# Identity products in TensorE's waits of a two-layer diffusion transformer with experts

## What is computed

```python
for l in range(2):                       # 256 latent tokens x, 256 context tokens xc, width 1024
    sh1, sc1, g1, sh2, sc2, g2 = modulation(c, w_ada[l], b_ada[l])      # silu(c) @ (1024 x 6144), also for c_ctx
    h_lat = rmsnorm(x, norm1_g[l]) * (1.0 + sc1) + sh1                  # the same for h_ctx
    o_lat, o_ctx = mixer(h_lat, h_ctx, ...)    # w_in; attention, 8 heads of 64; conv of 31 taps; w_out
    x = x + g1 * o_lat                   # xc likewise in layer 0 only
    h_lat = rmsnorm(x, norm2_g[l]) * (1.0 + sc2) + sh2
    f_lat = swiglu(h_lat, ...) if l == 0 else moe_swiglu(h_lat, ...)    # layer 1: top 2 of 8 experts
    x = x + g2 * f_lat
return rmsnorm(x, final_g)
```

## Time and profile before

| what | us |
|---|---|
| median of 3 runs | 1485.72 |
| lowest and highest | 1484.06 and 1485.72 |
| the profiled execution | 1484.85 |
| its span, first to last instruction | 1483.0 |
| TensorE busy in the span | 1384.1 |
| DMA rate over the span, GB/s | 266 |

### The profile page before, as it was taken

One profiled execution on the slowest core, in us unless ns is written; L12 is line 12 of the kernel. 1 busy time (PEld: TensorE's weight loads), 2 busy tenths in 40 slices (PEclk: granted clock), 3 DMA queues, 4 the chain that ended last, 5 costly groups with the idle time before them and its releaser, 6 DMA issues.

```text
span 1483.0 us, 25756 instructions
## 1 busy us (share of the span) xinstructions
PE 1384.1 (93%) x11327; PEld 821.8 (55%) x11327; DVE 525.7 (35%) x954; ACT 398.7 (27%) x701; POOL 4.1 (0%) x8
## 2 busy tenths in 40 slices
PE   6899889999999999989898999999999998889886
PEld 3688657888888888878675343333333332223221
DVE  2799884523232333469864112011100010001022
ACT  3522485422222322376482111010110010000001
POOL 0000000000000000000000000000000000000010
PEclk9999899999999999999999999999999999999898
DMA  9997903532331052411418999999999999999995
GB/s 353 385 343 274 352 2 114 171 114 68 103 114 57 29 187 97 143 57 58 171 41 341 399 371 409 406 409 406 409 407 408 408 406 410 405 410 406 408 410 221
DMA packets 147031, 395.92 MB, mean 267 GB/s; under 512 B 7488, under 2 KB 38752, under 8 KB 146912
## 3 DMA queue, kind: packets, MB, share of 16 engines
q1 hardware_dynamic: 144000, 388.86, 68.7%
q10 hardware_dynamic: 2336, 3.24, 0.6%
q0 software_dynamic: 576, 2.10, 0.4%
HBM read 390.76 MB, written 3.41 MB: 266 GB/s over the span
## 4 chain that ended last, share of the span: by engine, by line
PE 77%; DMA 12%; DVE 6%; SPq 2%; ACT 2%; issue 1%; DVEq 0%; ACTq 0%
PE bank L1196 22%; DMA weight_ring<-in_exp_w 9%; PE bank L1154 8%; PE bank L1013 5%; PE bank L1014 5%; PE bank L1012 5%; PE bank L735 4%; PE bank L736 4%; PE bank L737 4%; DMA weight_ring<-in_w_ada 3%; PE bank L1021 3%; PE bank L1022 3%; PE bank L1023 3%; PE bank L1162 2%; PE bank L681 2%; DVE weight_ring L1865 2%
## 5 line engine op out<-in xcount | busy, mean ns | idle before, releaser
L1196 PE MATMUL bank<-weight_ring,gathered 128*32 128x512 f32 (+1 forms) x3840 | 402.2, 569 | 32.9 <-DMA weight_ring<-in_exp_w 27.1
L1196 PEld LDWEIGHTS bank<-weight_ring,gathered 128*32 128x32 f32 x3840 | 127.0, 112 | 283.0 <-issue 282.3
L2259 DVE TENSOR_TENSOR scratch<-scratch,bank 64x512 f32<-64x512 f32 (+1 forms) x60 | 38.4, 640 | 357.2 <-ACT scratch L1672 354.9
L1154 PE MATMUL bank<-weight_ring,scratch 128*32 128x512 f32 x1344 | 157.8, 593 | 2.2 <-DMA weight_ring<-in_exp_w 2.2
L1014 PE MATMUL bank<-slot_halves,slot_halves 128*128 128x512 f32 x336 | 130.9, 390 | 0.0
L1013 PE MATMUL bank<-hT_halves,slot_halves 128*128 128x512 f32 x336 | 130.9, 390 | 0.0
L1012 PE MATMUL bank<-slot_halves 128*128 128x512 f32 x320 | 124.8, 390 | 0.0
L1865 DVE SCALAR_TENSOR_TENSOR weight_ring<-scratch,conv_weights,weight_ring 128x512 f32<-128x512 f32 (+1 forms) x207 | 121.3, 637 | 2.6 <-ACT weight_ring L1453 0.7
L736 PE MATMUL bank<-hT_halves,slot_halves 128*128 128x512 f32 (+1 forms) x352 | 122.0, 347 | 0.0
L735 PE MATMUL bank<-slot_halves,slot_halves 128*128 128x512 f32 (+1 forms) x284 | 105.6, 372 | 8.1 <-DVE slot_halves L1772 5.2
L1154 PEld LDWEIGHTS bank<-weight_ring,scratch 128*32 128x32 f32 x1344 | 43.8, 110 | 100.3 <-issue 91.0
(11 more groups left out here) (303 smaller groups left out, 1576.1 us busy)
## 6 DMA issues: line engine op xcount, KB each, us to landing
weight_ring<-in_exp_w SPq DMA_DIRECT2D x216, 1024.0 KB, 18.5
weight_ring<-in_w_ada SPq DMA_DIRECT2D x24, 2048.0 KB, 13.5
weight_ring<-in_exp_w SPq DMA_DIRECT2D x64, 768.0 KB, 15.0
weight_ring<-in_ffn_w SPq DMA_DIRECT2D x33, 1024.0 KB, 5.4
weight_ring<-in_w_in SPq DMA_DIRECT2D x8, 1024.0 KB, 11.6
weight_ring<-in_w_out SPq DMA_DIRECT2D x4, 2048.0 KB, 11.2
weight_ring<-in_w_in SPq DMA_DIRECT2D x2, 3072.0 KB, 15.2
expert_rows<-scratch ACTq DMA_DIRECT2D x14, 128.0 KB, 6.0
```

Of the source, the lines that this page charges most:

```text
L1154: i = mm(bank[6][quarter, :], at01[:, c0:c0 + BLOCK], w2[:, i_, half * 512:(half + 1) * 512], start=(first and i_ == 0), stop=(last and i_ ...
L1196: i = mm(ps[BLOCK * job:BLOCK * (job + 1), 0:cw], gathered_block(e, k, b), w[:, kk, a * cw:(a + 1) * cw], start=(k == 0), stop=(k == KT - 1))
```

## The change

A new function multiplies the 128 x 128 identity by itself into a PSUM bank that nobody reads; 105 such products stand at twelve places of TensorE's queue. Nothing waits for them and they wait for nothing, except that in the attention of both layers a wait on `roped` (third query or key tile rotated) stands ahead of them, since their bank held that tile's result. The other engines' queues are unchanged.

```diff
+            def keep_clock(n, ps):
+                for _ in range(n):
+                    mm(ps[:, 0:P], ident, ident, start=True, stop=True)
...
                     turn_first(1)
+                    keep_clock(9, bank[2])
                     first_modulation(3)
                     turn_first(2)
                     turn_first(3)
+                    keep_clock(18, bank[2])
                 else:
+                    keep_clock(6, bank[7])
                     norm_broadcast(4, TT)
+                    keep_clock(11, bank[7])
...
                 score(0)
                 for st in range(len(U) + 2):
+                    if st == 1:
+                        keep_clock(8, bank[4])
                     if st + 1 < len(U):
                         score(st + 1)
                     if st == 0:
+                        pe.wait_ge(m["roped"], 3)
+                        keep_clock(10 if l else 5, bank[4])
...
                         nk = 4 - U[p][2]
+                        if p == 0 and l == 0:
+                            keep_clock(7, bank[4])
...
+                if l:
+                    keep_clock(6, bank[7])
                 norm_broadcast(3 * l + 3, TQ)
+                if l:
+                    keep_clock(5, bank[7])
...
                 for u in range(ROW_UNITS[CH - 1]):
+                    keep_clock(3, bank[2])
                     second_unit(r, NG - 1, u)
```

## The result

The changed kernel takes 1486.8 us (median of 22 runs, 1483.6 to 1490.3); the kernel before, on the same chip, 1484.4 us (22 runs, 1482.8 to 1486.7). The ratio is 1.0016, 95% interval 1.0009 to 1.0022: it is **slower by 2.4 us**, where 1481.6 us were forecast and 1485.6 us was the upper end of the range. The profiled execution of after took 1485.67 us, its span is 1483.9 us.

What follows compares the result with a forecast made beforehand. It took DMA to bound the start and the experts' stream, with half-clock TensorE stretches costing time elsewhere; +1.4 + 0 - 1.25 - 1.8 - 0.7 - 0.9 = -3.25 us on 1484.85 gave 1481.6 us, range 1478.2 to 1485.6.

Steps and rivals of the forecast that it cites:

- The price of a product: All places: 0.225 us for each further product, up to 0.29 us each with the start, 0.45 us at half clock.
- rival C: All places: products don't hold the clock and are in the way at half clock; sum +5.2, 1490.0 us; chance 0.10.
- Start, +1.4 us: 9 and 18 products fit, but their lead ends at the w_ada transfer; half clock follows the new wait: +1.4 us.
- Rival A: Start: the clock holds behind the new wait at 71.45 us, start worth -0.3 us, total 1479.9 us; chance 0.17.
- rival B: Start: the early gain passes because the transfer lands sooner, -3.0 instead of +1.4, total 1477.2 us; chance 0.08.
- Attention of layer 0, 0 us: 5, 8, 7 products: gain at most 1.2 us, cost 0.6 us on VectorE's chain; taken as 0, bounds -0.6 and +0.8.
- rule against the forecast: Transposes don't engage the full clock; if identity products were treated alike, all gains would be nought.
- Entry to layer 1, -1.25 us: 6 and 11 products hidden in waits; the projection's first products reach ScalarE sooner: -1.25 us, bounds -1.4 and 0.
- Attention of layer 1, -1.8 us: 10 and 8 products hidden in waits; full clock brings the convolution's mean sooner: -1.8 us, bounds -2.4 and -0.6.
- Entry to the experts, -0.7 us: 6 and 5 products hidden in waits; the router's 32 records end sooner: -0.7 us, bounds -0.9 and 0.
- Tail, -0.9 us: 3 products ahead of each of the last four units remove half clock: -0.9 us, bounds -1.5 and +0.5.
- Rival D: Late places: products help, but dips move to other waits; half the late gains, 2.3, total 1483.9 us; chance 0.23.

Runs made afterwards that it cites:

- e2: The kernel before with only the 9 and 18 products of the start: 1487.6 us against 1484.2 us, ratio 1.0025.
- e9: The kernel before with 216 satisfied waits (108 instructions) in TensorE's idle places at the start, no products: 1487.1 us against 1484.6 us, ratio 1.0016.
- e3: The kernel before with only layer 0's 5, 8 and 7 attention products and their wait: 1487.2 us, ratio 1.0021.
- e7: e1 with 13 more products in layer 1's waits near 688 and 759 us: 1481.5 us against 1484.4 us, ratio 0.9981.
- e6: The kernel before with 108 satisfied waits (54 instructions) at the start, no products: 1483.9 us, ratio 1.0002.
- e1: The changed kernel with only the products of layer 1 and later, none at the start or in layer 0: 1483.7 us against 1484.2 us, ratio 0.9994.
- e4: The changed kernel with 14 more products ahead of the modulation that waits at 72 us: 1483.9 us, ratio 0.9996.
- e13: The kernel before with only the 12 products of the tail: 1485.1 us against 1483.8 us, ratio 1.0008.

## Why the prediction was wrong, step by step

- **The price of a product** was right: 18 products took 4.26 us, 9 took 2.25 us, 0.223 us for each further one, and behind them the stretches of the earlier trace rows are at 1.00, so rival C is out. ("Up to 0.29 us each with the start" misreads: two products in 0.71 us are 0.36 us each. Nothing rests on it.)
- **Start, +1.4 us.** Right in its steps: both groups fit, TensorE was ahead (2.3 us at 47 us, where 3.0 was forecast), nothing of it passed the transfer, a wait of 3.18 us opened and half clock stood behind it. By the ratios of e2 and e9, which share the number of instructions, the products of the start cost 1.3 us, with about 2 us to either side: the size is not confirmed. Rival A (the clock holds) happened in one of five traces, rival B in none.
- **Attention of layer 0, 0 us.** The last rotation came about 1.3 us later against its surroundings and the delay was gone at 186 us. e3 against e9 leaves 0.7 us, inside the bounds, and e3's pause is 0.7 us the longer one. In its rule against the forecast the prediction had transposes stay at half clock; in after eight of them ran at the full clock right behind the products, in 1.23 us, and in before another eight did in 1.09 us at 182.06 us, so the rule does not hold here:

```profile
176.00 1.23 PE L934 MATMUL bank<-constants,scratch 128*128 128x128 f32 x8
```

- **Entry to layer 1, -1.25 us.** In after -1.15 us: ScalarE's first convolution input at 664.05 us, 1.94 us later than in the earlier trace rows, where the program was 3.09 us late at the entry.
- **Attention of layer 1, -1.8 us.** In after -1.65 us; VectorE's wait for the mean fell from 2.46 us to 1.0 us, where 0.7 was forecast. The rows that answer to the earlier trace rows, the last of them for the entry to the experts:

```profile
728.30 0.70 PE L810 MATMUL bank<-scratch,constants 128*128 128x256 f32 x2
...
734.17 1.89 PE L942 MATMUL bank<-weight_ring,constants 128*128 128x256 f32 x8
...
792.06 3.19 PE L1070 MATMUL bank<-hT,router_w 128*8 128x128 f32 x32
```

- **Entry to the experts, -0.7 us.** The router's 32 records took 3.19 us, not 3.82, and ended 0.63 us sooner against the entry.
- **Experts.** DMA at 1.03 and 407 GB/s as forecast; leads and lags of before 830 us came out behind it, in e7 -2.75 and -2.6 us. They pass.
- **Tail, -0.9 us.** Open, see above; the step at fault is that a stretch seen in one trace was taken for the program's, where seven of nine traces without these products have none. The landings were misread as well: in e6 the last two units start 2.8 us apart, not 2.3.

**The step that failed first** is one that the part-by-part costing left out. The sum has a term for each product's time and none for the place of its instructions, which is to put it at nothing. Measured alone, on the kernel before, that term is +2.4 us (e9; 1.0 to 3.7 by its interval); in the three traces of after's program at that place the pause itself is 1.88, 1.82 and 0.99 us. **The second** is that the late gains were added up as if a stretch removed were gone: the sum gave them -4.65 us, e1 measured 0.9 us less than before (2.2 less to 0.4 more). Rival D had this mechanism and a chance of 0.23, but named other waits; the ones behind which stretches stood were the convolution's wait of 2.3 us at 688 us, the waits around 759 us and the one at 793 us, none of which the earlier trace rows show. Filling the first two gave 1.9 us back, with 1.9 us to either side. By the ratios the four pieces make 2.4 (pause) + 1.3 (start) + 0.7 (layer 0) - 0.9 (late) = 3.5 us against 2.4 us measured, the first and the last known to about 1.3 us and the two differences to about 2: the sum closes within the noise, and so would many others.

Of the forecast's own tests, "the gain at 47 us is still there at 162 us" did not happen, and no run of products ended after what it was to fill, except in the tail, where three of the four units in after start right behind them without a wait.

## What to carry to other kernels

Before filling TensorE's waits, list all of its waits of half a microsecond and more in the stage, and fill those ahead of work that nothing else holds back; a stretch at half clock that is removed at one wait can turn up behind the next. Leave a wait alone whose lead ends at a transfer that is due at a fixed time, or fill the wait that opens there too (e4). And count instructions: where a stage of short matmuls runs beside full DMA, look for TensorE's waits on "issue" and at the instruction queue's packets. Not every such wait is this one: all 17 traces have one of 1.45 us near 225 us and one of 4.4 to 4.6 us near 1378 us at the same instruction of the program, however many instructions stand ahead, and those were not looked into. And compare a candidate with the same kernel shifted by some tens of instructions before a loss or a gain of 0.15% is put down to the edit.

## What the runs showed of the hardware that was not expected

- TensorE ran out of instructions for up to 1.88 us in a stage that uses 256 of them in 4.7 to 5 us, with the DMA engines at 1.07 to 1.09. The block had arrived 1.34 to 1.51 us before it went on. Counted from 256 instructions before (number 5057), the transfer began 4.2 us later in after and 1.8 us later in before. Two weight pieces of 1 MB were under way in both; whether the fetch stood behind them or was asked for late wasn't tried.
- Where the stretches at half clock lie against the program differs from one execution to the next (the first one began between 15.4 and 17.8 us), so the same wait catches one or doesn't: 7 times in 13 at 688 us.
- A satisfied wait of TensorE took 0.053 us, two in one instruction of 0.106 us (54 of them in e6).
- Half clock in a DMA-bound stretch cost next to nothing in its place (from 870 to 1460 us before has 27 us of it and e13 17 us, and from 830 to 1466 us e13 gains 0.35 us on it), yet half clock or a pause ahead of such a stretch does cost, since the stream starts later: e9's 3.2 us at 796 us were 2.4 us at the end.
